# Five norm stages of a two-block network folded into the matrix products beside them

## The reference, cut to what matters

```
def rmsnorm(x, w):
    y = x * rsqrt(mean(x * x, axis=-1) + EPS)
    return y * w
```

## Time and profile before

| what | value |
|---|---|
| median of 3 runs | 4018.16 us (4016.17 to 4024.76) |
| the profiled execution's own time | 4016.14 us |
| its span, first to last instruction | 4014.3 us |
| mean granted TensorE clock | 0.909 of 2.4 GHz |
| PE busy | 3254.6 us (81%) |
| DVE busy | 2408.2 us (60%) |
| ACT busy | 1165.8 us (29%) |
| POOL busy | 938.1 us (23%) |
| instructions | 39723 |

### The profile page before, as it was taken

One profiled execution on the slowest core, in us unless ns is written; L12 is line 12 of the kernel. 1 busy time (PEld: TensorE's weight loads), 2 busy tenths in 40 slices (PEclk: granted clock), 3 DMA queues, 4 the chain that ended last, 5 costly groups with the idle time before them and its releaser, 6 DMA issues. The chain is left out here.

```text
span 4014.3 us, 39723 instructions
## 1 busy us (share of the span) xinstructions
PE 3254.6 (81%) x14144; PEld 2255.3 (56%) x14144; DVE 2408.2 (60%) x3257; ACT 1165.8 (29%) x1811; POOL 938.1 (23%) x791
## 2 busy tenths in 40 slices
PE   5899998759998927777778777777998778886698
PEld 1588776538896813333323333336886566775586
DVE  1556554659875495565566556545456356869564
ACT  1532122335434301111111111013454143444552
POOL 0000010010000066446545554520002036200100
PEclk8899998879998969999999999998999588998699
DMA  9557322019763489999999999974562053520163
GB/s 362 178 213 285 117 95 79 2 72 366 296 204 124 148 331 427 427 428 428 427 428 428 427 428 428 427 320 145 183 193 80 4 155 120 169 87 1 36 194 126
DMA packets 177467, 941.97 MB, mean 235 GB/s; under 512 B 22056, under 2 KB 27304, under 8 KB 99016
## 3 DMA queue, kind: packets, MB, share of 16 engines
q0 software_dynamic: 82944, 604.02, 36.2%
q1 hardware_dynamic: 94416, 336.66, 25.2%
HBM read 938.50 MB, written 2.10 MB: 234 GB/s over the span
## 5 line engine op out<-in xcount | busy, mean ns | idle before, releaser
L1487 PE MATMUL bank<-pe_v_rows,pe_diag 128*128 128x512 f32 x1920 | 901.9, 619 | 343.6 <-DMA pe_v_rows<-in_expert_v,pe_staged_v 200.6
L1487 PEld LDWEIGHTS bank<-pe_v_rows,pe_diag 128*128 128x128 f32 x1920 | 361.0, 196 | 883.9 <-issue 477.5
L1350 DVE SCALAR_TENSOR_TENSOR pe_junk<-pe_u_rows,h_rows 128x2048 f32<-128x2048 f32 x256 | 586.9, 2292 | 442.6 <-DMA pe_u_rows<-in_expert_u,pe_staged_u 431.2
L1295 POOL DMA_INDIRECT pe_u_rows<-in_expert_u,pe_staged_u x256 | 341.5, 1334 | 229.7 <-DVE pe_junk L1350 146.5
L1295 POOL DMA_INDIRECT pe_v_rows<-in_expert_v,pe_staged_v x248 | 316.6, 1277 | 327.9 <-PE bank L1487 269.6
L1448 ACT ACTIVATE pe_diag<-ident,pe_weights 128x128 f32<-128x128 f32 x240 | 91.8, 400 | 733.0 <-PE bank L1487 732.8
L246 PE MATMUL bank<-h_parts,b_top 128*128 128x512 f32 x768 | 274.4, 402 | 9.2 <-DVE b_rest L347 9.1
L347 DVE TENSOR_TENSOR in_rest<-in_ring,in_top 128x1024 fp32r<-128x1024 f32 x112 | 138.3, 1236 | 221.1 <-ACT in_top L316 220.9
L347 DVE TENSOR_TENSOR ab_rest<-ab_ring,ab_top 128x1024 fp32r<-128x1024 f32 x112 | 137.0, 1226 | 155.4 <-ACT ab_top L316 155.3
L347 DVE TENSOR_TENSOR c_rest<-c_ring,c_top 128x1024 fp32r<-128x1024 f32 x128 | 168.8, 1324 | 99.9 <-ACT c_top L316 99.3
L248 PE MATMUL bank<-h_parts,b_rest 128*128 128x256 f32 x768 | 216.9, 282 | 0.0
(11 more groups left out here) (512 smaller groups left out, 6421.5 us busy)
## 6 DMA issues: line engine op xcount, KB each, us to landing
b_ring<-in_w_mix SPq DMA_DIRECT2D x128, 512.0 KB, 5.6
in_ring<-in_w_in SPq DMA_DIRECT2D x112, 512.0 KB, 4.2
ab_ring<-in_w_ab SPq DMA_DIRECT2D x112, 512.0 KB, 4.1
mod_ring<-in_w_mod SPq DMA_DIRECT2D x32, 1024.0 KB, 7.9
v_rows<-in_w_mod POOLq DMA_DIRECT2D x32, 1024.0 KB, 5.7
k_cols<-in_w_mod POOLq DMA_DIRECT2D x32, 1024.0 KB, 7.9
c_ring<-in_w_c_in SPq DMA_DIRECT2D x64, 512.0 KB, 4.1
c_ring<-in_w_glu_out SPq DMA_DIRECT2D x64, 512.0 KB, 3.8
```

The source lines that it names most:

```text
L1295: gp.indirect_dma_start(buf[:, slot, :], None, table, bass.IndirectOffsetOnAxis(ap=staged[which][:, tile, e:e + 1], axis=0)).then_inc(sems ...
L1350: nc.vector.scalar_tensor_tensor(out=junk[:, :], in0=ub[:, s, :], scalar=1.0, in1=h2tm[:, tile, :], op0=ALU.mult, op1=ALU.mult, accum_out= ...
L1487: mm = nc.tensor.matmul(banks[4 * tile + b][:, :], diag[:, e % 4, :], vb[:, s, b * 512:(b + 1) * 512], start=False, stop=False, skip_group ...
```

## The change

All five norm stages go. In short:

- **Running squares.** In the products that write `xT` (the last 16 units of `mix`, `ab_out`, the last 16 of `glu`), ACT squares the tile of the unit before in each step and DVE adds it to a running total of 128x256 in the next. The last step does what is left.
- **Root and quarters in the next product.** `pq`, `c_in` and the last stage start with one matmul against ones, the root and its reciprocal; then the operand is scaled, shifted, cast and subtracted quarter by quarter. ACT casts two weight halves before the first quarter, DVE subtracts one weight half in each of the first two quarters.
- **Two norms are one.** In `ab` a `TwofoldNorm` takes sums of the weighed and of the plain squares and makes the operand of both norms at once: the scale is 1/sqrt(mean((x g)^2) + EPS (mean(x^2) + EPS)). The first norm is applied to `xT` one tile per unit, in units 1 to 16 on DVE. The narrow product moves from the head of TensorE's list to unit 4, and its four loads go on the SP queue in front of the weights; TensorE waits for them.
- **Copies in c_in.** Two of the four copies of a step go to ACT. GpSimd's chain also waits for the norm's matmul, since a table shares memory with the total.
- **Store by quarters** in the last stage, each as soon as its four tiles are scaled.
- All gains are loaded once, at the start.

```diff
@@ class SplitFirst
     def act_start(self, act, cast):
+        if self.norm:
+            self.norm.act_root(act)
+            cast()
+            cast()
         for q in range(4):
+            if self.norm:
+                self.norm.act_shift(act, q)
             self.operand.cast(act, q)
 
     def dve_start(self, dve, subtract):
+        if self.norm:
+            self.norm.dve_root(dve)
+            for q in range(4):
+                self.norm.dve_scale(dve, q)
+                if q < 2:
+                    subtract()
+                self.operand.subtract(dve, q)
+            return
...
+class RowNorm:
+    def pe(self, pe):
+        self.nc.tensor.matmul(self.bank[:, 0:T], self.ones, self.squares, start=True, stop=True).then_inc(self.summed, 1)
+
+    def act_root(self, act):
+        act.wait_ge(self.mean_done, 1)
+        self.nc.scalar.activation(self.root, self.root, ACT.Sqrt).then_inc(self.root_done, 1)
+
+    def dve_root(self, dve):
+        nc, link = self.nc, Chain(dve, self.chain)
+        if self.gain_of is not None:
+            link(nc.vector.scalar_tensor_tensor(out=self.gain, in0=self.gain_of, scalar=1.0, in1=self.gain, op0=ALU.add, op1=ALU.mult))
+        dve.wait_ge(self.summed, 1)
+        nc.vector.tensor_scalar(self.root, self.bank[:, 0:T], 1.0 / D, EPS, ALU.mult, ALU.add).then_inc(self.mean_done, 1)
+        dve.wait_ge(self.root_done, 1)
+        link(nc.vector.reciprocal(self.root, self.root))
+
+    def dve_scale(self, dve, q):
+        for k in range(4 * q, 4 * q + 4):
+            self.nc.vector.scalar_tensor_tensor(out=self.dst[:, k, :], in0=self.src[:, k, :], scalar=self.gain[:, k:k + 1], in1=self.root,
+                                                op0=ALU.mult, op1=ALU.mult).then_inc(self.scaled, 1)
+
+    def act_shift(self, act, q):
+        act.wait_ge(self.scaled, 4 * q + 4)
+        if self.shift is not None:
+            for k in range(4 * q, 4 * q + 4):
+                self.nc.scalar.activation(self.dst[:, k, :], self.dst[:, k, :], ACT.Identity, bias=self.shift[:, k:k + 1]).then_inc(self.shifted, 1)
+            act.wait_ge(self.shifted, 4 * q + 4)
+
+class TwofoldNorm(RowNorm):
+    def pe(self, pe):
+        for k in range(KT):
+            pe.wait_ge(self.weighed_done, k + 1)
+            self.nc.tensor.matmul(self.bank[:, 0:T], self.ones, self.weighed[:, k, :], start=(k == 0), stop=(k == KT - 1))
+        pe.wait_ge(self.folded, 1)
+        self.nc.tensor.matmul(self.plain_bank[:, 0:T], self.ones, self.squares, start=True, stop=True).then_inc(self.summed, 1)
+
+    def act_squares(self, act):
+        self.nc.scalar.activation(self.dst[:, 0:4, :], self.src[:, 0:4, :], ACT.Square).then_inc(self.squared, 1)
+        for k in range(KT):
+            self.nc.scalar.activation(self.weighed[:, k, :], self.src[:, k, :], ACT.Square, scale=self.first_gain[:, k:k + 1]).then_inc(self.weighed_done, 1)
+
+    def dve_root(self, dve):
...
+        for a in (4, 8, 12):
+            link(nc.vector.tensor_tensor(x2[:, a:a + 4, :], self.src[:, a:a + 4, :], self.src[:, a:a + 4, :], ALU.mult))
+        link(nc.vector.tensor_tensor(x2[:, 4:8, :], x2[:, 4:8, :], x2[:, 8:12, :], ALU.add))
+        link(nc.vector.tensor_tensor(x2[:, 4:8, :], x2[:, 4:8, :], x2[:, 12:16, :], ALU.add))
...
+        dve.wait_ge(self.summed, 1)
+        link(nc.vector.tensor_scalar(self.roots[:, 1, :], self.plain_bank[:, 0:T], 1.0 / D, EPS, ALU.mult, ALU.add))
+        link(nc.vector.tensor_single_scalar(self.root, self.roots[:, 1, :], EPS, ALU.mult))
+        nc.vector.scalar_tensor_tensor(out=self.root, in0=self.bank[:, 0:T], scalar=1.0 / D, in1=self.root, op0=ALU.mult, op1=ALU.add).then_inc(self.mean_done, 1)
...
+class RunningSquares:
+    def square(self, act, f):
...
+        act.wait_ge(self.written, RING + f + 1)
+        if f >= 4:
+            act.wait_ge(self.folded, f - 3)
+        self.nc.scalar.activation(self.squares[:, f % 4, :], self.src[:, f, :], ACT.Square).then_inc(self.squared, 1)
+
+    def add(self, dve, f):
...
+        dve.wait_ge(self.squared, f + 1)
...
+            self.nc.vector.tensor_tensor(self.total, self.total, self.squares[:, f % 4, :], ALU.add).then_inc(self.folded, 1)
+
+    def act_step(self, act, f):
+        self.square(act, f - 1)
+        if f == KT - 1:
+            self.square(act, f)
+
+    def dve_step(self, dve, f):
+        self.add(dve, f - 2)
+        if f == KT - 1:
+            self.add(dve, f - 1)
+            self.add(dve, f)
+            dve.wait_ge(self.folded, KT)
...
@@ last_norm_and_store
+            for q in range(4):
+                sp.wait_ge(norm.scaled, 4 * q + 4)
+                sp.dma_start(out[:, 4 * q:4 * q + 4, :], xT[:, 4 * q:4 * q + 4, :]).then_inc(stored, 16)
+            sp.wait_ge(stored, 64)
...
@@ class SplitAndLogs
-    def pe_start(self, pe):
+    def narrow(self, pe):
+        pe.wait_ge(self.operand.low_done, 4)
...
@@ class SplitAndPrepare
+            for s in range(2):
+                self.nc.scalar.activation(*self.steps_of(q, r, s), ACT.Copy).then_inc(self.stacked_act, 1)
...
-            for s in range(STEP):
+            for s in range(2, STEP):
...
+        gp.wait_ge(self.norm.summed, 1)
```

More of the change, by code:

```diff
@@ L158 @@
 class SplitFirst(Hooks):
+    norm = None
     def __init__(self, nc, name, source, high, low):
@@ L1126, in _, with __init__, bind @@
             turn_to_columns(pe, nc, banks, 0, parts, con, ready, turned, emptied)
[L1129 to L1141, removed]
+class RowNorm:
+    def __init__(self, nc, name, bank, src, dst, gain, con, root, squares, gain_of=None, shift=None):
+        self.nc, self.name, self.bank, self.src, self.dst, self.gain = nc, name, bank, src, dst, gain
+        self.ones, self.root, self.squares, self.gain_of, self.shift = con["ones"], root, squares, gain_of, shift
+    def bind(self, sem):
+        self.summed, self.mean_done, self.root_done = sem(f"{self.name}_summed"), sem(f"{self.name}_mean_done"), sem(f"{self.name}_root_done")
+        self.chain, self.scaled, self.shifted = sem(f"{self.name}_chain"), sem(f"{self.name}_scaled"), sem(f"{self.name}_shifted")
+    def pe(self, pe):
[21 more added lines that the diff above has]
+            act.wait_ge(self.shifted, 4 * q + 4)
@@ L1143, in _, with last_norm_and_store @@
+def last_norm_and_store(st, nc, banks, xT, norm, out):
+    with st.stage() as (block, sem):
+        norm.bind(sem)
+        stored = sem("out_stored")
         @block.sync
         def _(sp):
[L1145 to L1149, removed]
+            for q in range(4):
+                sp.wait_ge(norm.scaled, 4 * q + 4)
+                sp.dma_start(out[:, 4 * q:4 * q + 4, :], xT[:, 4 * q:4 * q + 4, :]).then_inc(stored, 16)
+            sp.wait_ge(stored, 64)
@@ L1151, in _ @@
         @block.scalar
         def _(act):
[L1153 to L1161, removed]
+            norm.act_root(act)
@@ L1163, in _ @@
         @block.tensor
         def _(pe):
[L1165 to L1169, removed]
+            norm.pe(pe)
         @block.vector
         def _(dve):
[L1173 to L1183, removed]
@@ L1184, in _ @@
-            dve.wait_ge(scaled, KT)
+            norm.dve_root(dve)
+            for q in range(4):
+                norm.dve_scale(dve, q)
+            dve.wait_ge(norm.scaled, KT)
 E8 = 8
@@ L1533, in bind, with act_start @@
         self.achain, self.chain = sem("gl_achain"), sem("gl_chain")
-        segments[1]["lead"] = self.widen
-        self.first = segments[1]["at"]
-    def pe_start(self, pe):
+        segments[1]["lead"], segments[2]["lead"] = self.narrow, self.widen
+        self.second, self.first = segments[1]["at"], segments[2]["at"]
+    def act_start(self, act, cast):
+        self.norm.act_squares(act)
+        super().act_start(act, cast)
+    def narrow(self, pe):
+        pe.wait_ge(self.operand.low_done, 4)
         narrow = self.small[0]
@@ L1963, in layer_ab @@
         stream(st, nc, "ab_out", t["w_ab_out"], [dict(kind="fm", n=16, cols=512, on="vector", both=lambda k: both_out[:, :, k, :], evac=add_to(nc, xT))],
-               stream_buffers(sb, "ab_out", own), banks, SplitAndStep(nc, t, "ab_out", h3, *out, tables, sb))
+               stream_buffers(sb, "ab_out", own), banks,
+               SplitAndStep(nc, t, "ab_out", h3, *out, tables, sb, RunningSquares(nc, "n4", xT, con["row_total"], sb("n4_squares", [P, 4, T]))))
 PAIRS = 64
@@ L1982, with __init__ @@
     uses_gp = True
-    def __init__(self, nc, t, name, source, high, low, tables, sb):
+    def __init__(self, nc, t, name, source, high, low, tables, sb, squares):
+        self.row_squares = squares
         super().__init__(nc, name, source, high, low)
@@ L2459, with __init__ @@
     uses_gp = True
-    def __init__(self, nc, ug, parts, sig, out):
+    def __init__(self, nc, ug, parts, sig, out, squares):
         super().__init__(nc, "glu", ug, *parts)
+        self.row_squares = squares
         self.nc, self.ug, self.sig, self.out = nc, ug, sig, out
```

149 lines of the change are left out of this document (110 added, 39 removed).

## The result

The changed kernel takes **3995.24 us** (median of 5 runs, 3990.48 to 4002.93), the kernel before in the same comparison 4017.48 us (4013.59 to 4024.76). The ratio is 0.9946, 95% interval [0.9934, 0.9958]: 22 us faster (17 to 27). The direction was forecast, the size was not: 41 us were expected, and 3995.24 lies above the range of 3962 to 3992. The profiled execution has a span of 4000.3 us against 4014.3.

What follows compares the result with a forecast made beforehand. Norm stages leave TensorE idle in gaps before three products, and nothing overlaps the last norm. Terms sum to -41.3 us: 4016.14 profiled becomes 3974.8, plus 2.0 to the median gives 3976.9 us; range 3962 to 3992.

Steps and rivals of the forecast that it cites:

- -3.8 - 12.3 - 8.2 - 7 - 10.4 + 0.4 = -41.3 us: Whole kernel: gains at pq, ab, c_in's start, c_in's copies and the end, less one more small load at the head.
- The starts themselves: First units of pq, ab and c_in end 32, 36 and 26 us behind the old last instruction of the stage in front.
- a first root later than 4 us: Sign of being wrong at a norm's start: the root was priced ready 3.8 us after the stage in front.
- pq: Start of pq: first unit after 31.95 us against 35.8, quarters serial; -3.8 us, bounds -1 to -7.
- What a gap loses is won in full: At the three product starts: after a first unit the stream runs at TensorE's pace, so shortening the gap gains fully.
- ab: Start of ab: gap 56.0 to 36.5 us, less 7.2 us for the unhidden narrow product; -12.3 us, bounds -8 to -17.
- c_in: Start of c_in -8.2 us (bounds -5 to -11); two copies moved to ACT -7 us (bounds 0 to -13).
- End: Last norm and store: root, quarters of scaling, stores under the scaling; -10.4 us, bounds -9 to -12.
- Contention eats more: Rival: c_in copies give nothing, adds cost GpSimd 3 us more, pq gives 1; 28 us saved, 3990; 20%.
- my 2: End of ab_out: DVE adds beside GpSimd cost from nothing to some 5 us; 2 us taken.
- A drain behind the table loads: Root table loads at pq, c_in and end: a 1.38 us drain would lose some 4 us; forecast spoke against it.
- the slow stream: Rival: TensorE, fed in bursts, stays at 1.2 GHz in the following stream; all 32 c_in units make 4131 us; 2%.

Runs made afterwards that it cites:

- a2: The kernel before with the two new SBUF tiles (1408 bytes) allocated but unused; 4039.4 us, ratio 1.0054.
- aligned profile: Profile of the changed kernel with the gains tile at 8 columns instead of 6, shifting later tiles by 1536 bytes, not 1408; 3980.47 us, ratio 0.9900.
- c2: The changed kernel with padded gains tile, DVE scaling the next quarter before subtracting this one at the three starts; 3965.16 us, ratio 0.9877.
- c4: The changed kernel with padded gains tile, all four c_in copies on ScalarE, next quarter scaled first, narrow product between ab's first quarters; 3961.29 us, ratio 0.9861.
- b4: The changed kernel with padded gains tile and all four copies of a c_in unit back on DVE; 3988.83 us, ratio 0.9924.
- c3: The changed kernel with padded gains tile, narrow product four by four behind the quarters of ab's first unit; 3980.07 us, ratio 0.9906.

## Why the prediction was wrong

- **The failed step** is the sum itself, "-3.8 - 12.3 - 8.2 - 7 - 10.4 + 0.4 = -41.3 us": a term is missing. It took the expert stage as it stood in the trace of before and has no cost for the new tiles, and none of the rivals has a stage that the diff doesn't touch get slower. The placement of two tiles, 1408 bytes together, cost 17 us there (a2: 21 us in the whole), nearly all of the 18.3 us between 3976.9 and 3995.24. With 128 bytes of padding the same change gives 3980.5, 3.6 from the 3976.9 forecast and inside the range, and 34 to 47 us of gain against 41.3.
- **The starts themselves** came out as forecast: the first units of `pq`, `ab` and `c_in` ended 32.7, 35.8 and 26.1 us behind the old last instruction of the stage in front, where 32, 36 and 26 were given. One sign of being wrong did show, a first root later than 4 us: in `pq` the reciprocal is done 4.5 us behind the stage in front, not 3.8, mostly by the matmul of 1.19 us.
- **pq**: right mechanism, 1.9 us of the 3.8 (0.2 in the aligned profile). Within the bounds of 1 to 7 in the first, below them in the second. "What a gap loses is won in full" is not exact: the first unit came 3.2 us sooner, but the stretch behind it takes 84.2 to 87.1 us over the fourteen profiles, with either kernel. Six profiles with the norm stages and six with the change (c2 and c4 left out) differ by 1.2 us on average over `pq`.
- **ab**: 13.5 us against 12.3; small loads, sum and the 7.2 us of the narrow product each within 0.5 us of their value.
- **c_in**: 14.1 us against 15.2 for start and copies, 9.0 of them by the end of the first unit (8.2 forecast) and 5.2 behind it (7 forecast). The split is of one pair of profiles: in the aligned profile it is 9.9 and 6.7, and the first to last evacuation of `c_in` alone takes 185.6 to 190.1 us over six profiles with the norm stages. Inside the new kernel the copies are worth 11.5 us (b4).
- **End**: 10.2 against 10.4.
- **The rivals.** "Contention eats more" would give 3990 and looks confirmed by the total; it isn't: its copies gave 11.5 us inside the new kernel, not nothing, and GpSimd was 0.6 us beyond my 2, not 3. A total near a rival's number is no evidence for that rival. A drain behind the table loads did not occur. In `pq` of the changed kernel the granted clock fell back once, to a mean of 0.66 between 1310 and 1315 us, around the end of the first unit, and is 1.00 from 1315 us on; in `ab` it is 1.00 from 2756 us and in `c_in` from 3371 us on, both before the first unit ends. So the slow stream did not come.

## What to carry to other kernels

Where a stage is bound by transfers with all DMA engines full, print the start byte of the tiles they land in and keep it at a multiple of 256: any tile allocated ahead of them moves it, and 64 bytes can cost half of what a whole optimisation earns (20.8 us here by the medians, against 38.0 for the aligned change). When a change alters memory, compare the stages that it does not touch first. When work is cut into pieces that two engines share, the order on the busier one (next piece ahead of finishing this one) can be worth more than the cut itself: in `pq` 7.7 us to the first evacuation, where the change had won 1.9.

## What the runs showed of the hardware

- Gathers of 8 KB rows into SBUF: 427 GB/s and 309 ns a packet when the destination starts on a multiple of 256 bytes, 421 to 422 GB/s and 314 ns when it starts 64 or 128 past one; no difference between 64 and 128.
- The one stream compared that doesn't fill the DMA engines doesn't feel it: the ring of the first product starts 128 past a multiple in the kernel before and on one in the changed kernel, and its subtractions stretch over 523.2 and 522.2 us (521.3 to 523.6 over the fourteen profiles).
- An add of two SBUF operands on DVE took 0.49 us alone and 0.98 beside GpSimd; ScalarE's copies took 0.64 to 0.68 us each, beside it and after it.
- The same work can be granted a different clock in another execution: between `c_in` and the end of `glu` 0.836 in c3's profile (437.4 us), 0.855 to 0.863 in the thirteen others (421.3 to 426.5 us). Whether the spread of 10 us between a kernel's runs comes from this is not shown.
